# Row stages handed over by token halves: closing tiles in half order, norm weights beside the squares, factors with the addition to h

## The reference

```python
h = h + rms_norm(mix @ w_out, post_mix_norm)              # OUT
u = rms_norm(h, pre_mlp_norm) @ w_mlp_up
h = h + rms_norm(square(relu(u)) @ w_mlp_down, post_mlp_norm)   # MLP, 4096 wide
e = rms_norm(p @ w_ple_proj, ple_norm)                    # PLE, 256 wide
h = h + e * sigmoid(h @ w_ple_gate)                       # GATE
proj = rms_norm(h, norm_mix) @ w_in_2                     # IN2, 2560 columns
h = h + [rms_norm(y_sc), rms_norm(y_cf)] @ w_out_2        # OUT2
q = rms_norm(h, norm_ffn) @ w_q                           # WQ, then PEER
h = h + (gelu(hn @ u.T) * gates) @ v                      # 16384 experts, dense
out = rms_norm(h, final_norm)
```

## Time and profile before

| what | value |
|---|---|
| median of 3 runs | 1487.34 us (1485.51 to 1487.4) |
| the profiled execution's own time | 1485.99 us |
| its span in the profile | 1484.2 us |
| mean granted clock of TensorE | 0.963 of 2.4 GHz |
| TensorE busy | 1359.1 us, 92% |
| VectorE, ScalarE, GpSimd busy | 883.6, 783.3, 400.5 us |
| transfers | 226.16 MB, mean 152 GB/s |

### The profile page before, as it was taken

One profiled execution on the slowest core, in us unless ns is written; L12 is line 12 of the kernel. 1 busy time (PEld: TensorE's weight loads), 2 busy tenths in 40 slices (PEclk: granted clock), 3 DMA queues, 4 the chain that ended last, 5 costly groups with the idle time before them and its releaser, 6 DMA issues.

```text
span 1484.2 us, 26169 instructions
## 1 busy us (share of the span) xinstructions
PE 1359.1 (92%) x8942; PEld 1238.1 (83%) x8942; DVE 883.6 (60%) x1647; ACT 783.3 (53%) x1377; POOL 400.5 (27%) x215
## 2 busy tenths in 40 slices
PE   4999955999987776699999999999999999999996
PEld 4998944999976775599999999999988888888885
DVE  3677354666555777568997155566625555555554
ACT  4646223444444542446777666666645555555553
POOL 0101200000000382004888866666660000000000
PEclk9999977999998898799999999999999999999998
DMA  6533003555553242344555544444445555555553
GB/s 232 173 121 115 15 28 121 184 185 186 195 172 118 83 139 85 99 143 157 184 185 182 184 146 142 142 142 143 142 157 172 189 191 184 184 187 189 188 185 127
DMA packets 61988, 226.16 MB, mean 152 GB/s; under 512 B 7120, under 2 KB 7504, under 8 KB 61536
## 3 DMA queue, kind: packets, MB, share of 16 engines
q1 hardware_dynamic: 60176, 219.18, 42.8%
q10 hardware_dynamic: 1744, 6.07, 1.1%
HBM read 224.18 MB, written 1.05 MB: 152 GB/s over the span
## 4 chain that ended last, share of the span: by engine, by line
PE 87%; DVE 5%; POOL 3%; ACT 2%; issue 2%; DMA 1%; ACTq 0%; DVEq 0%; POOLq 0%
PE bank L488 76%; PE bank L875 4%; POOL arena L1345 1%; DVE arena L1710 1%; ACT arena L918 1%; PE bank L538 1%; PE bank L463 1%; PE bank L659 1%; PE bank L669 1%; PE bank L667 1%; DMA arena<-in_meta 1%; DVE arena L1430 1%; ACT w_hi L945 1%; PE bank L828 0%; PE bank L681 0%
## 5 line engine op out<-in xcount | busy, mean ns | idle before, releaser
L945 ACT ACTIVATE w_hi<-ring 128x1024 fp32r<-128x1024 f32 x416 | 441.2, 1061 | 551.2 <-PE bank L488 383.3
L1416 DVE TENSOR_TENSOR w_lo<-ring,w_hi 128x1024 fp32r<-128x1024 f32 x276 | 340.5, 1234 | 343.1 <-ACT w_hi L945 334.2
L488 PE MATMUL bank<-hT_hi,w_hi 128*128 128x256 f32 (+2 forms) x1728 | 431.8, 287 | 3.4 <-ACT w_hi L945 1.7
L488 PE MATMUL bank<-hT_lo,w_hi 128*128 128x256 f32 (+2 forms) x1728 | 423.7, 283 | 0.0
L1372 POOL TENSOR_TENSOR w_lo<-ring,w_hi 128x1024 fp32r<-128x1024 f32 x128 | 310.4, 2427 | 172.3 <-ACT w_hi L945 172.0
L488 PEld LDWEIGHTS bank<-hT_hi,w_hi 128*128 128x128 f32 x1728 | 327.8, 190 | 6.3 <-ACT w_hi L945 3.2
L488 PEld LDWEIGHTS bank<-hT_lo,w_hi 128*128 128x128 f32 x1728 | 328.8, 190 | 0.2
L488 PE MATMUL bank<-hT_hi,w_lo 128*128 128x256 f32 (+2 forms) x1728 | 239.7, 281 | 5.8 <-POOL w_lo L1354 5.8
L488 PEld LDWEIGHTS bank<-hT_hi,w_lo 128*128 128x128 f32 x1728 | 220.2, 189 | 6.2 <-POOL w_lo L1354 6.2
L488 PE MATMUL bank<-w_hi,wgt_hi 128*128 128x512 f32 x512 | 203.5, 398 | 2.3 <-DVE wgt_lo L1948 2.3
L488 PE MATMUL bank<-w_hi,wgt_lo 128*128 128x512 f32 x512 | 203.4, 397 | 0.0
(11 more groups left out here) (290 smaller groups left out, 1646.6 us busy)
## 6 DMA issues: line engine op xcount, KB each, us to landing
ring<-in_stream SPq DMA_DIRECT2D x416, 512.0 KB, 3.2
arena<-in_rows ACTq DMA_DIRECT2D x1, 1536.0 KB, 17.2
consts<-in_consts ACTq DMA_DIRECT2D x1, 1152.0 KB, 12.6
h<-in_x ACTq DMA_DIRECT2D x1, 1024.0 KB, 7.4
arena<-in_keys ACTq DMA_DIRECT2D x1, 1024.0 KB, 5.0
out_h<-arena SPq DMA_DIRECT2D x1, 1024.0 KB, 4.1
arena<-in_rows ACTq DMA_DIRECT2D x1, 512.0 KB, 3.7
arena<-in_pT ACTq DMA_DIRECT2D x1, 256.0 KB, 5.2
```

The source lines that it names most:

```text
L488: mm = nc.tensor.matmul(o, a, b, start=first and not low_part and xp is x[0], stop=last and low_part)
L945: nc.scalar.activation(w_hi[:, g % S, :], ring[:, g % R, :], ACT.Copy).then_inc(hi_done, 1)
L1416: nc.vector.tensor_tensor(w_lo[:, g % S, :], ring[:, g % R, :], w_hi[:, g % S, :].bitcast(F32), ALU.subtract).then_inc(lo_done, 1)
```

## The change

A passage is cut by token halves, and its row work is rearranged.

- The last two row tiles of OUT, MLP, GATE and PEER run in another order (closing_rows): all 12 matmuls of both tiles for half 0, then rows_half is raised, then all 12 for half 1. Both tiles' high parts, and for PEER all weights' splits, are needed at its start. OUT2 does so with its last tile alone. The closing products of zeros are gone; MLP's opening ones go ahead of the transposes, which for MLP now use banks 4 to 7, and MLP's first block waits block by block (in every round, since it is in the loop). The last round of MLP and of PEER is written out after its loop.
- squares takes one half; each activation waits for the one before. Where it reads banks, VectorE multiplies the other column half by the norm weights at that time (weighted), and the two change places. The factor is then applied in the addition to h (add_scaled).
- inv_rms goes by halves: add epsilon to the first column sum, add the second, power, on one column each. The squares are scaled by 1/sqrt(1024) inside the activation.
- normalise and the gating ahead of OUT go by halves and column halves, and TensorE transposes each four blocks as they come.
- The next stage's two high and low parts are made behind the squares and around the normalising. p is split while MLP's last tiles run. PLE's first tile stands ahead of h's transposes and its second one behind them; PLE's squares and weighting stand between GATE's parts; GATE goes to banks 0 to 3. Sigmoid, gate product and addition go by quarters.
- PEER's first two weights are split while its first half ends. The final weight row is loaded four tiles before the end. The output is stored in four parts of 256 KB, two each by SyncE and ScalarE. The two tiles of padding are gone.

The diff, cut to its core:

```diff
+            for g in range(G_END // R * R, G_END):
+                sp_eng.wait_ge(lo_done, g - R + 1)
+                sp_eng.dma_start(ring[:, g % R, :], stream_in[g]).then_inc(slot_full[g % R], 16)
+            for t in range(NT):
+                sp_eng.wait_ge(out_ready, t + 1)
+                sp_eng.dma_start(out[0, t * P:(t + 1) * P, 0:HALF], normed[:, t, 0:HALF]).then_inc(out_done, 16)
...
+            def closing_rows(tiles, b0, first=False, halves_done=True):
+                for t in range(NT):
+                    for j, ((slot, low), lhs) in enumerate(tiles):
+                        for c in range(2):
+                            for x in lhs[t]:
+                                mm = nc.tensor.matmul(bank[b0 + 2 * t + c][:, :], x, w_hi[:, slot, c * HALF:(c + 1) * HALF],
+                                                      start=False, stop=False)
+                        if t:
+                            mm.then_inc(hi_used, 1)
+                        pe.wait_ge(lo_done, low)
...
+                        if t:
+                            mm.then_inc(tiles_done, 1)
+                    if t == 0:
+                        mm.then_inc(rows_half, 1)
...
-            open_sums(False).then_inc(mlp_full, 1)
...
+            row_tile(tile(G_PLE), lambda t: p_lhs(0, t), 4, True, False)
+            pe.wait_ge(weighted_done, 8)
+            pe.wait_ge(ssq_done, 4 * 3 + 4)
             transposes(3)
-            pe.wait_ge(scaled_out, 12)
-            rows_out(G_GATE, 8, hT_lhs, 4, stage=3)
+            row_tile(tile(G_PLE + 1), lambda t: p_lhs(1, t), 4, False, True)
+            hT_block(3, KD - 1)
+            rows_out(G_GATE, 8, hT_lhs, 0, stage=3)
...
+            last = [tile(G_V + n) for n in (N_KEYS - 2, N_KEYS - 1)]
+            pe.wait_ge(wgt_out, N_KEYS)
+            closing_rows([(w, [wgt_lhs(j, t) for t in range(NT)]) for j, w in enumerate(last)], 0)
...
-            his(G_OUT, 8)
+            his(G_OUT, 6)
+            act.wait_ge(rows_half, 1)
+            squares(1, 0, banks_of(4, 0))
             act.wait_ge(tiles_done, G_OUT + 8)
-            squares(1, [bank[4 + q][:, :] for q in range(4)])
-            squares(2, halves(h), 2)
+            squares(1, 1, banks_of(4, 1))
+            for t in range(NT):
+                squares(2, t, h_halves(t), 0)
+            his(G_OUT + 6, 2)
...
+            squares(3, 0, banks_of(0, 0))
+            his(G_PLE - 2, 1)
+            act.wait_ge(tiles_done, G_PLE)
+            squares(3, 1, banks_of(0, 1))
+            his(G_PLE - 1, 1)
+            his(G_PLE, 1)
+            blocks_out(3)
...
-            his(G_OUT2 + 4, 4)
-            squares(6, halves(h), 8)
+            his(G_OUT2 + 4, 3)
+            for t in range(NT):
+                squares(6, t, h_halves(t), 12)
+            his(G_OUT2 + 7, 1)
...
+                for t in range(NT):
+                    pool.wait_ge(ssq_done, 4 * n + 2 * t + 1)
+                    link(nc.gpsimd.tensor_scalar(ms[n % 2][:, t:t + 1], q[:, t, 0:1], EPS, None, ALU.add))
+                    pool.wait_ge(ssq_done, 4 * n + 2 * t + 2)
+                    link(nc.gpsimd.tensor_tensor(ms[n % 2][:, t:t + 1], ms[n % 2][:, t:t + 1], q[:, t, 1:2], ALU.add))
+                    nc.gpsimd.tensor_tensor(rstd[n % 2][:, t:t + 1], ms[n % 2][:, t:t + 1], neghalf[:, 0:1], ALU.pow)\
+                        .then_inc(rstd_done, 1)
...
+            def weighted(n, b0, row, dst, t):
+                for c in (1, 0):
+                    if c == 0:
+                        dve.wait_ge(ssq_done, 4 * n + 2 * t + 1)
+                    o = slice(c * HALF, (c + 1) * HALF)
+                    nc.vector.tensor_tensor(dst[:, t, o], bank[b0 + 2 * t + c][:, :], rows[:, row, o], ALU.mult)\
+                        .then_inc(weighted_done, 1)
...
+            def add_scaled(n, src, t):
+                dve.wait_ge(weighted_done, weights[0])
+                dve.wait_ge(rstd_done, 2 * n + t + 1)
...
+            los(G_OUT, 6)
+            dve.wait_ge(rows_half, 1)
+            weighted(1, 4, 0, post, 0)
+            add_scaled(1, post, 0)
+            dve.wait_ge(tiles_done, G_OUT + 8)
+            weighted(1, 4, 0, post, 1)
+            add_scaled(1, post, 1)
+            dve.wait_ge(added, 4)
+            normalise(2)
+            los(G_OUT + 6, 1)
             blocks_out(2)
+            los(G_OUT + 7, 1)
```

More of the change, by code:

```diff
@@ L58 @@
 G_END = G_PEER + 2 * N_KEYS
-PAD = 2
 PEER_BODY = 4
@@ L701, in _, with open_sums, mid_lhs, mlp_round @@
             rows_out(G_OUT, 8, hT_lhs, 4, stage=1)
-            transposes(2)
             pe.wait_ge(zeroed, 1)
             zb = zeros[:, :].bitcast(BF16)
-            def open_sums(opening):
+            def open_sums():
                 for b in range(4):
-                    mm = nc.tensor.matmul(bank[b][:, :], zb, zb.unsqueeze(1).to_broadcast([P, HALF // P, P]),
-                                          start=opening, stop=not opening)
-                return mm
-            hT_block(2, KD - 1)
-            open_sums(True)
-            with pe.Fori(0, MLP_ROUNDS) as i:
+                    nc.tensor.matmul(bank[b][:, :], zb, zb.unsqueeze(1).to_broadcast([P, HALF // P, P]),
+                                     start=True, stop=False)
+            open_sums()
+            transposes(2)
+            def mid_lhs(m, t):
+                return mid_hi[:, m, t * P:(t + 1) * P], mid_lo[:, m, t * P:(t + 1) * P]
+            def mlp_round(i, closing):
                 for m in range(8):
@@ L908, in link, with squares, h_halves, banks_of @@
                 act.wait_ge(act_step, steps[0])
-            def squares(n, halves, updates=None):
-                if n:
-                    act.wait_ge(ssq_done, 4 * n)
-                for q, a in enumerate(halves):
-                    if updates and q % 2 == 0:
-                        act.wait_ge(added, updates - 1 + q // 2)
-                    nc.scalar.activation(normed[:, q // 2, (q % 2) * HALF:(q % 2 + 1) * HALF], a, ACT.Square,
+            def squares(n, t, halves, updates=None):
+                for c, a in enumerate(halves):
+                    q = 2 * t + c
+                    if updates is None and n and c:
+                        act.wait_ge(weighted_done, weighted_at[n] + 2 * t + 1)
+                    if updates is not None:
+                        act.wait_ge(added, updates + q + 1)
+                    if n or q:
+                        act.wait_ge(ssq_done, 4 * n + q)
+                    nc.scalar.activation(normed[:, t, c * HALF:(c + 1) * HALF], a, ACT.Square, scale=D ** -0.5,
                                          accum_out=ssq[n % 2][:, q:q + 1]).then_inc(ssq_done, 1)
+            def h_halves(t):
+                return [h[:, t, c * HALF:(c + 1) * HALF] for c in range(2)]
+            def banks_of(b0, t):
+                return [bank[b0 + 2 * t + c][:, :] for c in range(2)]
             def his(g0, n):
@@ L924, in his @@
                     hi(g + S)
-            def halves(buf):
-                return [buf[:, t, c * HALF:(c + 1) * HALF] for t in range(NT) for c in range(2)]
             def blocks_out(n):
@@ L1094, in _, with mlp_round @@
             blocks_out(2)
-            with act.Fori(0, MLP_ROUNDS) as i:
+            def mlp_round(i, closing):
                 for m in range(8):
@@ L1678, in _ @@
             nc.vector.memset(upad[:, :, 0:14], 0.0)
-            dve.wait_ge(added, 6)
-            normalise(5, 4)
+            dve.wait_ge(added, 12)
+            normalise(5)
+            los(G_GATE + 6, 1)
             blocks_out(4)
+            los(G_GATE + 7, 1)
             dve.wait_ge(tr_lo, KD * 5)
```

300 lines of the change are left out of this document (177 added, 123 removed).

## The result

The kernel after took 1450.19 us (median of 4 runs, 1449.18 to 1452.48), the kernel before 1487.09 beside it (4 runs): a ratio of 0.9759, 95% interval [0.9745, 0.9774]. The forecast was 1449.0 in 1443 to 1459. In a later series the unchanged kernel after gave 0.9764 [0.975, 0.9777]. The profiled execution has a span of 1448.8 against 1484.2.

What follows compares the result with a forecast made beforehand. TensorE holds 87% of the chain; the rest is mainly passages between row stages, a relay of engines without overlap. 10.4+18.1+2.3+0.6-0.4+3.6+2.8 = 37.4; 1485.99-37.4 = 1448.6, given as 1449, forecast 1444 to 1453 (chance 0.62), stated range 1443 to 1459.

Steps and rivals of the forecast that it cites:

- OUT to MLP: Passage from OUT's end to MLP's first product: that product at 244.77 against 255.13, gain 10.4 us.
- the rival of a slow one-column power: GpSimd's power on one column takes 1.22 us, not 0.70; with small stalls 1453 to 1458 us, chance 0.15.
- GpSimd's power over 1 us: Sign named beforehand that would show the forecast wrong, in GpSimd's power on one column, taken as 0.70 us.
- MLP to IN2: Passages from MLP over PLE and GATE to IN2: IN2's first product at 477.0 against 495.06, gain 18.1 us.
- The sigmoid's table load stands behind its wait: GATE to IN2: the 1.28 us load begins at 464.7, over before half 1 arrives, so three quarters stop counting.
- OUT2 to WQ: Passage from OUT2 to WQ: normalising starts at 623.75 in place of 625.75; with finer pieces, gain 2.3 us.
- Gating in halves: Ahead of OUT: the gating is cut into halves of 0.62 in place of 1.24, gain 0.6 us.
- Start: Kernel's start: four chained squares (4 x 0.17 longer), then the meta rows' power, partly offset by GpSimd's shorter rest: -0.4 us.
- Between PEER's halves: Weights 0 and 1 split early: TensorE goes on at 1106.5, not 1108.82, first tile 2.81, not 4.07: gain 3.6 us.
- The end: Program's end: closing order gives back 2.0 waiting for weight 127; smaller last store; gain 2.0 or 3.7, taken 2.8 us.
- The dear case: At the end: half clock follows TensorE's gap, half 1 at 1474.2 rather than 1472.5, so gain 2.0, not 3.7.
- The rival of half clock: 1.2 GHz in PLE's second tile, two GATE tiles and V's last half costs 5 to 11: 1454 to 1460, chance 0.14.

Runs made afterwards that it cites:

- the second profile: Profile of the kernel after run once more with no edit: 1451.82 us, ratio 0.9764 to the kernel before, OUT's first product at 210.67.
- the zeros: Kernel after with five more rounds of four products of zeros behind OUT's last product, in the wait ahead of MLP: 1448.9 us, ratio 0.9742 to the kernel before.
- the early split alone: Kernel before with only PEER's second-half weights 0 and 1 split behind the third of the last GELUs: 1483.02 us against 1486.77, ratio 0.9978.
- one closing tile: Kernel after with PEER's second half closing with one tile by token halves instead of two: 1447.44 us, ratio 0.974 to the kernel before.

## Why the prediction was right

The time, 1449.0 for 1450.19, and its course are those forecast: the relay is cut by halves, and the halves overlap. The single terms are less exact than the time. In the spans the gain is 35.4 for 37.4. Of the 2.0 that are missing 1.4 are the clock's fall at 185, which the second profile doesn't have, and 1.1 the end; the other errors are smaller and offset each other, and that part is luck. By its own steps:

- **OUT to MLP**, 10.4: 10.0. The relay by halves runs as followed there, half 1's weighting late behind VectorE among it. The power was 0.58, below the 0.70 taken, so the rival of a slow one-column power falls. The 1.22 in the earlier trace rows that carried it starts beside a TENSOR_SCALAR of VectorE (L1398, 16.87 to 18.29 in that trace) and ends at 18.32, 0.03 after it. In after, where VectorE's operations beside it are shorter, the same power takes 0.67: it was held up, not slow. Its sign, "GpSimd's power over 1 us", is there once even so, the last power of the program with 1.44, and for the same reason.
- **MLP to IN2**, 18.1: 17.8, out of errors that offset each other. "The sigmoid's table load stands behind its wait" is wrong: it ran at 453.88, 3 us ahead, and GATE's half 0 to IN2's first product was some 10.9 for 12.3 forecast. The earlier trace rows can't tell: there the load follows the last high part (to 479.08) within 0.02, but TensorE had ended at 478.85, so it fits both readings. Against it, MLP's first product to GATE's took 190.98 for the 190.07 followed there (445.2 less 255.13): MLP's start is at half clock for 4.3 us where before had 1.9, which I hadn't followed and which the zeros price at 1.3 to 1.5 in all. And GATE's half 0 took 20.3 from its first product for 19.5, 0.36 of it the gap ahead of the closing tiles. GATE at full clock, where before starts it at half, lies in the 18.1 without being named.
- **OUT2 to WQ**, 2.3: 2.5. The low part ahead of the normalising is as forecast, and was the largest thing left in this passage.
- **Gating in halves**, 0.6: 0.61 in the second profile. **Start**, -0.4: +0.2. The chained squares cost 0.4 (2.98 from the start of the first to the end of the last, for 2.57) and not 0.7, and the meta rows' power, which stands on the path, fell from 1.22 to 0.67:

```profile
17.49 0.67 POOL L1400 TENSOR_TENSOR mstat<-mstat,consts 16x1 f32<-16x1 f32 x1
```

- **Between PEER's halves**, 3.6: 4.05 in the profile of the early split alone, 3.3 in its times.
- **The end**, "2.0 or 3.7, I take 2.8": 1.7. The dear case came. The second half is 3.7 longer than with the early split alone (363.93 for 360.20), the gap of 1.95 and the fall of the clock, of which I had left open whether it comes; the forecast's later end of half 1, 1474.2 for 1470.46, is 3.7 as well. The clock fell among the closing products in every profile with the gap but one, that of the zeros ahead of MLP (362.38, so the gap is worth 2.2 and the clock 1.5 over the 360.21 of one closing tile), and in none without. Against that the end is 5.4 shorter.
- **The rival of half clock** was right in its last named place (V's last half), wrong in PLE and GATE, which run at full pace in after (granted clock 1.00 from 426 to 464), and it missed MLP's start.

What no run settles: the stretches repeat only to 0.5, and IN2 to WQ to more (131.86 to 134.05 in kernels alike there), so terms below that are read from rows, not shown by times.

## What to carry to other kernels

Closing a row stage by halves is worth one half of the closing products, here 2.3 us a passage with two closing tiles, where the next work is a relay between engines; where the closing order must wait for its operands it gives that back, and one closing tile is better than two. What stands in a queue ahead of a half's first operation can cost its wait and not only its length, so it goes behind: 2.6 us ahead of WQ, though nothing ahead of GATE. The products behind a passage can run at the lower clock, and a shorter passage can leave more of them there, 4.3 us for 1.9 at MLP; products of zeros in the wait gave that back, 1.3 to 1.5 us.

## What I had not expected of the hardware

- GpSimd's short operations are held up by VectorE's with both operands in SBUF: 0.22 becomes 1.09, 0.57 becomes 1.44, and each ends 0.08 to 0.44 after VectorE's. A TENSOR_SCALAR of VectorE in SBUF holds them too, 0.76 for 0.57, and 1.22 for 0.67 in the earlier trace rows. In the kernel before the engines took turns, and it lay on the path at the start alone; work in halves makes them meet.
- One kernel's two executions differ by 1.4 us in an untouched stage, by a stretch at 1.2 GHz that begins at 185 in one and not in the other.
- The sigmoid's table load ran ahead of the wait of the ACTIVATE that needs it: 1.28 us, hidden. Not all do. In PEER, as in the earlier trace rows, some stand behind a wait in after too; what decides it no run here tells.

```profile
701.19 1.28 ACT L1003 ACT_TABLE_LOAD   x1 [0.55 <-POOL w_lo L1467]
```

- Stores of 256 KB land in 2.1 and 2.5 us (the page of after, part 6), below the 2.75 drawn from the earlier trace rows.
